# Mamba segment sums as differences of running sums on 32-row groups, in a decoder trunk on one Trainium2 core

## What is computed

```python
xbc = jax.nn.silu(causal_depthwise_conv(xbc, conv_w, conv_b))   # 4 taps, 1024 channels
xs, bm, cm = jnp.split(xbc, [M2_W, M2_W + M2_G * M2_N], axis=-1)
dt = jax.nn.softplus(dt_raw + dt_bias); a = -jnp.exp(a_log)
a_cum = jnp.cumsum(dt * a)                                       # per head, over tokens
seg = a_cum[..., :, None] - a_cum[..., None, :]
lmat = masked_exp(seg, causal)                                   # decay from token s to token l
y = ((cm @ bm^T) * lmat) @ (xs * dt) + d_skip * xs               # 8 heads of 64
y = rms_norm(y * silu(z), norm_w)                                # groups of 256
```

## Time and profile before

| | |
|---|---|
| median of 3 runs | 1523.17 us (1521.41 to 1523.21) |
| the profiled execution | 1521.63 us |
| its span, first to last instruction | 1519.4 us |
| mean granted TensorE clock | 0.995 of 2.4 GHz |
| PE busy | 1473.7 us, 97% |
| DVE busy | 1182.5 us, 78% |
| ACT busy | 932.6 us, 61% |
| POOL busy | 52.6 us, 3% |
| DMA | 388.46 MB, 256 GB/s over the span |

### The profile page before, as it was taken

How to read it: one execution, slowest core, us unless ns; L and a number is a source line. 1 busy time by engine, 2 the same in 40 slices (tenths; PEclk the granted TensorE clock), 3 DMA queues, 4 the chain that set the end, 5 groups by cost and what they waited for, 6 DMA issues and landing times.

```text
span 1519.4 us, 21593 instructions
## 1 busy us (share of the span) xinstructions
PE 1473.7 (97%) x8363; PEld 1281.3 (84%) x8363; DVE 1182.5 (78%) x1159; ACT 932.6 (61%) x936; POOL 52.6 (3%) x58
## 2 busy tenths in 40 slices
PE   8999999999999999998999999999999999999996
PEld 7989897999888989896788887888878888888884
DVE  6886655555437886646998988989989899898996
ACT  6645344444337543454777777777777777777773
POOL 0031000000000131000000000000000000000000
PEclk9999999999999999999999999999999999999998
DMA  7432443455546432544699998999899999999993
GB/s 307 141 137 100 152 164 129 149 191 172 192 156 230 143 112 84 194 139 166 240 360 380 350 352 341 353 377 360 342 343 352 375 363 341 362 351 374 364 360 125
DMA packets 54481, 388.46 MB, mean 256 GB/s; under 512 B 6000, under 2 KB 6256, under 8 KB 8176
## 3 DMA queue, kind: packets, MB, share of 16 engines
q1 hardware_dynamic: 53840, 384.98, 67.9%
q10 hardware_dynamic: 544, 2.10, 0.3%
HBM read 386.00 MB, written 1.05 MB: 255 GB/s over the span
## 4 chain that ended last, share of the span: by engine, by line
issue 53%; PE 41%; DVE 4%; DMA 1%; ACT 1%; POOL 0%; DVEq 0%; POOLq 0%; ACTq 0%
PE pb L1014 11%; PE pb L1016 11%; PE pb L1015 11%; PE pb L1233 1%; PE pb L1253 1%; DVE wlo L1527 1%; DMA arena<-in_mem 1%; DVE arena L1801 1%; PE pb L1155 1%; PE pb L995 1%; DVE arena L1694 1%; PE pb L1199 0%; DVE xTl L1576 0%; DMA h<-in_x 0%; DVE arena L1786 0%
## 5 line engine op out<-in xcount | busy, mean ns | idle before, releaser
L2093 DVE TENSOR_TENSOR wlo<-raw,whi 128x2048 fp32r<-128x2048 f32 x175 | 400.5, 2291 | 50.5 <-ACT whi L926 48.6
L926 ACT ACTIVATE whi<-raw 128x2048 fp32r<-128x2048 f32 x175 | 335.8, 1920 | 134.6 <-PE pb L1016 134.6
L1527 DVE TENSOR_TENSOR wlo<-raw,whi 128x2048 fp32r<-128x2048 f32 (+1 forms) x101 | 226.6, 2255 | 132.1 <-ACT whi L591 131.7
L1014 PE MATMUL pb<-whi,mTh 128*128 128x512 f32 x768 | 305.2, 397 | 4.2 <-DVE kvXr L2093 3.3
L591 ACT ACTIVATE whi<-raw 128x2048 fp32r<-128x2048 f32 (+1 forms) x101 | 190.0, 1884 | 180.1 <-PE pb L1016 175.0
L1016 PE MATMUL pb<-whi,mTl 128*128 128x512 f32 x768 | 300.1, 391 | 0.0
L1014 PE MATMUL pb<-xTh,whi 128*128 128x256 f32 x736 | 210.3, 286 | 2.7 <-DVE xTl L1564 1.2
L2093 DVE TENSOR_TENSOR kvXr<-kvX,whi 128x2048 fp32r<-128x2048 f32 x86 | 196.7, 2291 | 19.1 <-ACT whi L926 17.7
L1015 PE MATMUL pb<-xTl,whi 128*128 128x256 f32 x736 | 208.6, 283 | 0.0
L1016 PE MATMUL pb<-xTh,wlo 128*128 128x256 f32 x736 | 208.6, 283 | 0.0
L1015 PE MATMUL pb<-wlo,mTh 128*128 128x512 f32 x528 | 205.6, 389 | 0.0
(11 more groups left out here) (330 smaller groups left out, 2203.5 us busy)
## 6 DMA issues: line engine op xcount, KB each, us to landing
raw<-in_ffn_w SPq DMA_DIRECT2D x209, 1024.0 KB, 4.8
kvX<-in_ffn_w SPq DMA_DIRECT2D x88, 1024.0 KB, 4.9
raw<-in_lin_w SPq DMA_DIRECT2D x64, 1024.0 KB, 4.8
raw<-in_lin_w SPq DMA_DIRECT2D x4, 536.0 KB, 5.1
arena<-in_mem ACTq DMA_DIRECT2D x2, 1024.0 KB, 8.5
h<-in_x SPq DMA_DIRECT2D x1, 1024.0 KB, 4.9
out<-xn SPq DMA_DIRECT2D x2, 512.0 KB, 2.7
consts<-in_con SPq DMA_DIRECT2D x1, 836.0 KB, 13.1
```

Of the source, the lines that this page charges most:

```text
L926: nc.scalar.activation(whi[:, (MOE0 + c) % HRING, :], xraw_slots[c % XRING], ACT.Copy).then_inc(hi_ready, 1)
L1014: nc.tensor.matmul(o, lh, rh, start=first, stop=False)
L1527: V.tensor_tensor(wlo[:, m % RING, c], raw[:, m % RING, c], whi[:, m % HRING, c].bitcast(F32), ALU.subtract).then_inc(lo_ready, 1)
L2093: V.tensor_tensor(xlo_slots[c % XRING], xraw_slots[c % XRING], whi[:, (MOE0 + c) % HRING, :].bitcast(F32), ALU.subtract).then_inc(lo_ready, 1)
```

## The change

The segment sum from s to l is now the difference of two running sums. Once per layer, behind L1122, PE forms running sums for all heads: `Wm` holds the logarithms of head i of a round in columns 32i and 32i+1, and four products with the tables "after" and "upto" give the sums in rows 32i and 32i+1 of bank 7. ACT makes two operands of them: `Qm` with the sum in row 32i and a one in row 32i+1, `Km` with a one in row 32i and the negated sum in row 32i+1 (a new table "units" of three columns holds the factors). A round of segment sums (`segments`) is now eight products on row groups of 32: four of 256 columns and four of 128, each on the 32 rows of its head. A difference can come out slightly above zero. DVE therefore takes the minimum with zero over the two triangular blocks in PSUM (`nonpositive`) before ACT's `Exp`. `ALm` and `ABm` are gone.

The steps of the stage are set anew between the chunks, on PE as follows:

| | before | changed |
|---|---|---|
| behind chunk 15 | B by C, tokens turned | round 0 |
| then | round 0 | chunk 16 |
| then | chunk 16 | B by C, tokens turned |
| then | round 1 | chunk 17 |
| then | chunk 17 | round 1, chunk 18 |
| then | outputs, turn | outputs, turn |
| then | chunks 18, 19, 20 | chunks 19, 20 |

Tap 3 of the convolution, with the bias, moves from DVE to ACT (`last_tap`): for the first half behind the copy of xbc0, for the second behind the exponentials of level 3.

```diff
@@ ACT
                 ins.then_inc(fox_p, 1)
+                act.wait_ge(m2_c, layer + 1)
+                even, odd, less = (const("units")[:, i:i + 1] for i in range(3))
+                sums = pb[:, 7, :].rearrange("p (r s) -> p r s", r=2)
+                nc.scalar.activation(Qm, sums, ACT.Identity, scale=even, bias=odd)
+                nc.scalar.activation(Km, sums, ACT.Identity, scale=less, bias=even).then_inc(m2_rows, 1)
...
+                def last_tap(i):
+
+                    cw, cb = par_("conv_w", layer), par_("conv_b", layer)
+                    act.wait_ge(lin_act, evac_count((f"xbc{i}", layer)))
+                    for c in range(4 * i, 4 * i + 4):
+                        ins = nc.scalar.activation(xcv[:, c, :], xraw[:, c, 3:3 + S], ACT.Identity,
+                                                   scale=cw[:, 4 * c + 3:4 * c + 4], bias=cb[:, c:c + 1])
+                    ins.then_inc(conv_tap, 1)
...
-                split_to(last_chunk(layer, "xk0") + 2)
+
+                def decays(r):
+
+                    act.wait_ge(m2_neg, 2 * layer + r + 1)
+                    nc.scalar.activation(Mm[:, 4 * r:4 * r + 4, :], pb[:, 4:8, 0:3 * P], ACT.Exp).then_inc(m2_e, 1)
+
+                decays(0)
+                take("xk0", layer, (tiles(kX[:, 0:4, :]), 0, 512, ACT.Copy, 1.0, None))
                 act.wait_ge(m2_t, layer + 1)
                 nc.scalar.activation(xs, pb[:, 6:8, :], ACT.Copy).then_inc(m2_xs, 1)
-                take("xk0", layer, (tiles(kX[:, 0:4, :]), 0, 512, ACT.Copy, 1.0, None))
...
+                split_to(chunk0(layer, "xk1") + HRING)
+                decays(1)
                 take("xk1", layer, (tiles(kX[:, 4:8, :]), 0, 512, ACT.Copy, 1.0, None))
@@ PE
                 mm.then_inc(fox_pt, 1)
+                pe.wait_ge(m2_w, layer + 1)
+                for rnd in range(2):
+                    o = pb[:, 7, rnd * S:(rnd + 1) * S]
+                    nc.tensor.matmul(o[:, 0:P], Wm[:, 0, rnd, :], const("after"), start=True, stop=True)
+                    mm = nc.tensor.matmul(o[:, P:S], Wm[:, 1, rnd, :], upto, start=True, stop=True)
+                mm.then_inc(m2_c, 1)
...
+                def segments(rnd):
+
+                    for i in range(4):
+                        r = slice(32 * i, 32 * i + 32)
+                        nc.tensor.matmul(pb[:, 4 + i, 0:2 * P], Km[r, rnd, 0:P], Qm[r, rnd, :], start=True, stop=True)
+                    for i in range(4):
+                        r = slice(32 * i, 32 * i + 32)
+                        mm = nc.tensor.matmul(pb[:, 4 + i, 2 * P:3 * P], Km[r, rnd, P:S], Qm[r, rnd, P:S], start=True,
+                                              stop=True)
+                    mm.then_inc(m2_seg, 1)
+
+                pe.wait_ge(hg_ok, layer + 1)
+                segments(0)
+                project("xk1", layer, M, (0,))
                 pe.wait_ge(xcv_ready, layer + 1)
-                pe.wait_ge(hg_ok, layer + 1)
+                pe.wait_ge(m2_e, 2 * layer + 1)
...
-                for rnd in range(2):
-                    if rnd:
-                        project("xk1", layer, M, (0,))
-                        pe.wait_ge(m2_e, 2 * layer + 1)
-                    for i in range(4):
...
-                project("xk1", layer, M, (1,))
+                segments(1)
+                project("xv0", layer, M, (0,))
                 pe.wait_ge(m2_m, 2 * layer + 2)
...
-                project("xv0", layer, M)
+                project("xv0", layer, M, (1,))
@@ DVE, the formation of Wm and the stage
+                for t in range(NT):
+                    at = Wm[:, t, :, :].rearrange("p r (i x) -> p r i x", x=32)[:, :, :, 0:2]
+                    log = A12[:, t, 4:12].rearrange("p (r i) -> p r i", r=2).unsqueeze(3).to_broadcast([P, 2, 4, 2])
+                    ins = V.tensor_scalar(at, log, 2.0 * t - 1.0, None, ALU.mult)
+                ins.then_inc(m2_w, 1)
...
+                def nonpositive(rnd):
+
+                    dve.wait_ge(m2_seg, 2 * layer + rnd + 1)
+                    own = pb[:, 4:8, 0:3 * P].rearrange("p b (i s) -> p b i s", i=3)[:, :, 0:3:2, :]
+                    V.tensor_scalar(own, own, 0.0, None, ALU.min).then_inc(m2_neg, 1)
```

More of the change, by code:

```diff
@@ L90 @@
 for _name, _w in (("ident", P), ("minus_half", 20), ("neg", P), ("upto", P), ("ones", P), ("after", P), ("m2mask", 3 * P),
-                  ("before", P), ("restart", 2 * S), ("iota", P), ("pair", NE)):
+                  ("before", P), ("restart", 2 * S), ("iota", P), ("pair", NE), ("units", 3)):
     CCOL[_name] = (_n, _n + _w)
@@ L368, in build @@
         m2_cb = sem("m2_cb")
-        m2_a = sem("m2_a")
+        m2_w = sem("m2_w")
+        m2_c = sem("m2_c")
+        m2_rows = sem("m2_rows")
         m2_seg = sem("m2_seg")
+        m2_neg = sem("m2_neg")
         m2_e = sem("m2_e")
@@ L782, in _ @@
                 take("z", layer, (zs, 0, 512, ACT.Silu, 1.0, None))
-                split_to(last_chunk(layer, "xk0") + 2)
+                def decays(r):
[3 more added lines that the diff above has]
+                take("xk0", layer, (tiles(kX[:, 0:4, :]), 0, 512, ACT.Copy, 1.0, None))
                 act.wait_ge(m2_t, layer + 1)
                 nc.scalar.activation(xs, pb[:, 6:8, :], ACT.Copy).then_inc(m2_xs, 1)
-                take("xk0", layer, (tiles(kX[:, 0:4, :]), 0, 512, ACT.Copy, 1.0, None))
-                for r in range(2):
-                    act.wait_ge(m2_seg, 2 * layer + r + 1)
-                    nc.scalar.activation(Mm[:, 4 * r:4 * r + 4, :], pb[:, 4:8, 0:3 * P], ACT.Exp).then_inc(m2_e, 1)
-                    if r == 1:
-                        split_to(chunk0(layer, "xk1") + HRING)
+                split_to(chunk0(layer, "xk1") + HRING)
+                decays(1)
                 take("xk1", layer, (tiles(kX[:, 4:8, :]), 0, 512, ACT.Copy, 1.0, None))
@@ L1127, in _ @@
                 project("xbc1", layer, X, (0,))
+                pe.wait_ge(m2_rows, layer + 1)
                 pe.wait_ge(fox_ptc, layer + 1)
@@ L1685, in convolve @@
                     dve.wait_ge(lin_act, evac_count((f"xbc{half}", layer)))
[L1686 removed]
+                    dve.wait_ge(conv_tap, 2 * layer + half + 1)
+                    for tap in (2, 1, 0):
                         for c in range(4 * half, 4 * half + 4):
[L1688 to L1691 removed]
+                            if tap < 2:
                                 dve.wait_ge(dve_c, chain[0] - 3)
[L1694 to L1696 removed]
+                            ins = V.scalar_tensor_tensor(out=xcv[:, c, :], in0=xraw[:, c, tap:tap + S],
+                                                         scalar=cw[:, 4 * c + tap:4 * c + tap + 1],
+                                                         in1=xcv[:, c, :], op0=ALU.mult, op1=ALU.add)
                             chain[0] += 1
@@ L1812, in _ @@
                 split_to(chunk0(layer, "z") + HRING)
-                V.tensor_copy(ABm, bc(A12[:, 1, 4:12], P))
-                for t in range(NT):
-                    ins = V.tensor_tensor(ALm[:, t, :, :], const("after").unsqueeze(1).to_broadcast([P, M2_H, P]),
-                                          bc(A12[:, t, 4:12], P), ALU.mult)
-                ins.then_inc(m2_a, 1)
                 dve.wait_ge(hg_o, layer + 1)
@@ L1824, in _ @@
                 heads = xn[:, :, 0:512]
+                def nonpositive(rnd):
+                    dve.wait_ge(m2_seg, 2 * layer + rnd + 1)
+                    own = pb[:, 4:8, 0:3 * P].rearrange("p b (i s) -> p b i s", i=3)[:, :, 0:3:2, :]
+                    V.tensor_scalar(own, own, 0.0, None, ALU.min).then_inc(m2_neg, 1)
                 after("z", layer)
+                dve.wait_ge(hg_ok, layer + 1)
+                link(V.tensor_tensor(sqh, heads, heads, ALU.mult))
+                link(V.tensor_reduce(ss[:, :, 0:8], sqh.rearrange("p t (h d) -> p t h d", d=DH), AX.X, ALU.add))
+                V.tensor_scalar(ss[:, :, 0:8], ss[:, :, 0:8], 1.0 / DH, EPS, ALU.mult, ALU.add).then_inc(ss_ready, 1)
+                nonpositive(0)
+                after("xk0", layer)
                 dve.wait_ge(m2_t, layer + 1)
@@ L1828, in _ @@
                                 ALU.mult).then_inc(m2_cb, 1)
-                after("xk0", layer)
                 dve.wait_ge(m2_xs, layer + 1)
@@ L1836, in _, with decayed @@
                                     bc(par_("m2_d", layer), DH), ALU.mult)
-                dve.wait_ge(hg_ok, layer + 1)
-                link(V.tensor_tensor(sqh, heads, heads, ALU.mult))
-                link(V.tensor_reduce(ss[:, :, 0:8], sqh.rearrange("p t (h d) -> p t h d", d=DH), AX.X, ALU.add))
-                V.tensor_scalar(ss[:, :, 0:8], ss[:, :, 0:8], 1.0 / DH, EPS, ALU.mult, ALU.add).then_inc(ss_ready, 1)
-                dve.wait_ge(m2_cb, layer + 1)
-                for rnd in range(2):
+                def decayed(rnd):
                     dve.wait_ge(m2_e, 2 * layer + rnd + 1)
@@ L1846, in _ @@
                                     ALU.mult).then_inc(m2_m, 1)
```

(6 more changed lines are left out.)

31 lines of the change are left out of this document (13 added, 18 removed).

## The result

The changed kernel takes 1532.24 us (median of 4 runs, 1530.81 to 1534.7), against 1523.19 for the kernel before in the same comparison (1521.41 to 1523.95). The ratio is 1.0058 with a 95% interval of 1.0045 to 1.0071. That is 9 us slower, where I forecast 0.6 us faster and a range that ended at 1528.5. The profiled execution took 1530.81 us with a span of 1528.5 us. Its mean granted clock is 0.990 against 0.995 before. The other executions say the same: 0.983 to 0.986 in the three that were not profiled, and never under 0.991 in the kernel before, in the comparisons that follow.

The account below looks back on a forecast made before the run. PE, busy 97% of the span, and its short waits bound the kernel. Of some 6.9 us saved per layer, 2.5 and 4.1 return as waits, leaving 0.6 for both layers: 1522.6 us, range 1518.5 to 1528.5.

Parts of the forecast that it names:

- PE's own work: Segment rounds on PE: two fall from 7.1 to 2.2 us, running sums add 0.9; 4.0 us saved per layer.
- The minimum: DVE's minimum with zero in PSUM after each round, put at 1.21 us, with 0.71 and 1.76 as ends.
- the table load: ACT's table load before the segment rounds' exponentials; claimed to cost nothing, since it does not wait for their operands.
- The chain through the stage: From round 0 to the outputs: DVE's list without a gap makes PE wait 2.5 us, outputs starting at 149.8.
- the chunk that is no longer there: Behind the outputs: with chunk 18 moved ahead, PE waits 4.1 us for chunk 20's remainder; chunk 20 at 165.5.
- Rival (2): Front of the chain dearer: row groups not running side by side or minima at 1.76; 1524.8 to 1527.8, chance 0.14.
- Rival (3): DVE not in the way, so waits shrink or vanish: 1520.6, 1517.6 or some 1509; chance 0.12 in all.
- its last case: Waits before the outputs and at chunk 20 both vanish, PE's savings stay whole: some 1509, chance 0.02.
- the sum: Whole kernel: 0.3 us earlier per layer, 0.6 for both, median 1522.6.
- rival (1): PE's clock falls in the new waits: one fall gives 1524.3, one in each layer 1526.0; chance 0.22 in all.
- The tap: Tap 3 moved to ACT at the convolution: DVE's level 4 operands 0.79 us earlier, the stage begins 0.79 earlier.
- Running sums elsewhere: DVE's operations for `Wm` and ACT's `Qm` and `Km`, about 0.6 us each, hidden at no cost; 1.2 us if uncovered.

Follow-up runs that it names:

- the second: The changed kernel with DVE's minimum of round 1 moved straight behind the decays of round 0; 1528.13 us.
- third run: The changed kernel with DVE's remainder of chunk 20 moved ahead of the skip term and its minimum of round 1 behind round 0's decays; 1518.55 us.
- the first run: The changed kernel with DVE's remainder of chunk 20 moved ahead of the skip term, before its wait for PE's outputs; 1525.48 us.

## Why the prediction was wrong

**PE's own work** was right. A round takes 0.86 us (126.03 to the first product of chunk 16 at 126.89); I had put 1.1 and kept 0.8 as an end. The estimate by the Trainium skill ("TensorE: Matmul & The Clock Gate", Measured speedup vs the span model) was 0.86. The trace agrees with its 3.07 times, in single precision as well. The minimum took 1.23 (1.21 put), and the table load ran at 119.34, nine microseconds ahead of the exponentials at 128.30, and cost nothing:

```profile
119.34 1.28 ACT L814 ACT_TABLE_LOAD   x1
128.30 1.45 ACT L814 ACTIVATE arena<-pb 128x1536 f32<-128x1536 f32 x1 [7.67 <-DVE pb L1868]
```

**The chain through the stage** and **the chunk that is no longer there** were right to some tenths: outputs at 149.62 (149.8 forecast) behind a wait of 2.25 (2.5), remainder of chunk 20 begun at 163.11, the wait there 3.92 (4.1), chunk 20 at 165.49 (165.5). The stage began at 126.03, 0.3 later than put. Rival (2), a dearer front, is out: round and minimum cost what was put. Rival (3) did not come about in this kernel. But its last case, savings whole at "some 1509", is what the reordered DVE list gave: 1510.7.

**The failed step is the sum.** It took each wait at its length (2.5 and 4.1 us) and put the half clock behind them at nothing. That was left to rival (1) with 0.22. What the runs showed in its place are falls of 1.7 and 5.1 us behind these waits in the profiled execution, and 8.2 us that came back when the waits were filled. Rival (1) is what happened in kind, but its figure for one fall in each layer, 1526.0, was 6 us too low. Two things in it were mis-sized.

*The chance.* I looked for one point between 1.28 and 4.1 us, and gave the whole rival 0.22. There is no such point. The runs show falls at waits of 1.48 us (one layer each of the second and third run), of 2.25 (five of six: layer 1 of the changed kernel, both layers when it ran once more, both of the first run), of 2.46 (chunk 20 in layer 0 of the changed kernel once more), and at all six of 3.5 us or more. They also show waits of 1.48, 1.7, 2.25 and 2.63 us without one. There were two candidates in each layer, not one. The trace of the kernel before already had a fall close above the 1.28: its one fall, that of the earlier trace rows, began half a microsecond behind a wait of 1.37 us,

```profile
265.92 1.51 PE L1007 MATMUL pb<-consts,xn 128*128 128x128 f32 x8 [1.37 <-DVE xn L1595]
```

while two waits of 1.6 us in its experts' part had none behind them. The Trainium skill ("TensorE: Matmul & The Clock Gate", Why this matters for your kernels) was cited beside this rival with its rule that idle gaps between bursts of matmuls bring the clock back to half, and the rule deserved more weight than it got. The traces agree with it in kind: each run that kept unfilled waits of 1.48 us or more in the stage had a fall at one of them. They differ in size, since the Trainium skill names there only gaps longer than the 1.48 and 2.25 us behind which falls came here; for those the measurement decides.

*The price.* I took 1.7 us a fall from the earlier trace rows and so got 1526.0 for one in each layer. A fall at chunk 20 did cost 1.7 in layer 0 (up to 3.4 in layer 1 of the old kernel with a wait put in). A fall at the outputs cost 5.1, and up to 6.8 in other runs, because the clock stayed down for 10 to 14 us, over most of the outputs (products of 64 columns) and the turn, and came back only in the chunk behind them. I had not asked what PE does behind each wait. That what PE runs there sets the length of a fall fits the stage in all profiles, but no run changed it by itself. The price also falls on the path in full: DVE's skip term waits for the outputs (9.25 us idle in layer 1 against 5.67 in layer 0), and chunk 20 waits for DVE:

```profile
607.40 1.22 DVE L1909 TENSOR_TENSOR xn<-arena,pb 128x1024 f32<-128x1024 f32 x1 [9.25 <-PE pb L1251]
```

There the wait of 3.9 shrinks to 2.6, so the net cost of layer 1's fall is 3.8.

Even the row that the 1.7 came from misled. The stretch of the earlier trace rows had no fall in the changed kernel's execution, and what follows came no sooner for it: the lag of 1.45 us that the changed kernel brought from layer 0 is still 1.45 at 439 us. The fall cost the kernel before nothing in the end. PE waits for DVE's `xTl` there, 0.37 us with the fall and 0.80 without, which covers a part; what covers the rest is open.

**Account of the 9.2 us** (profiled executions, changed less before). Layer 0: -0.3 from the new order and +1.7 from the fall, together the lag of 1.45. Layer 1: +3.7 (-0.3, +5.1, less 1.3 of wait that the fall covered, and 0.2 of rounding and small change). Two falls in the experts' part bring 1.4 and 1.6, and waits there for the remainders kept in SBUF (`kvXr`, 4.2 us against 3.3) the rest. The fall at 1128 us stands behind one of these waits, of 1.8 us. Why the clock falls in the experts' part in one execution and not in another stays open. The profiles of the kernel before and of the tap alone have none there; every other one, with or without the change, has one to three.

**The tap** gained, as forecast, though the stage began only 0.5 us earlier for 0.8. **Running sums elsewhere**, `Qm` and `Km` at 0.78 each (0.6 put), were hidden, as forecast.

## What to carry to other kernels

When a reordering leaves PE a wait of 1.5 us or more without a matmul, price it as the wait plus half of the time that PE may then spend at 1.2 GHz, and ask that for every such wait. Here that time was 3.4 to 6.8 us where products of 512 columns came next, and 10 to 14 us where the outputs and a turn did. A fall may also stay out, so this is the upper end. Before giving up a gain in arithmetic that came with such an order, look for idle time on the engine that is late: here three moved lines of DVE turned 1532 us into 1511. Where no order helps, a few needless products in the wait are cheap, but look in the trace for new stops elsewhere: 16 small products brought two here, and 4 large ones none.

## What was not expected of the hardware

- The half clock outlasts its cause. PE was busy without a gap from 598.21 on, and yet stayed at 1.2 GHz to about 610, through 64-column products and transposes; behind chunk 20, where 512-column products follow, it took 3.4 to 6.8 us in the runs.
- The same wait of 2.25 us brought a fall in one layer and none in the other, in one execution. So did the wait of 1.48 us in the third run.
- With 16 needless products of 128 columns in each layer of the old kernel, PE's stream stopped twice for 2.5 us, some 320 and 520 us behind the second group; with 4 of 512 columns it did not, nor did it in the changed kernel with 24 of 128. The cause is open.
- Products on four 32-row groups in single precision ran 3.07 times as fast as one after the other (0.86 us for twelve units of 0.22).
